# Hybrid two-layer decoder trunk on one core: where the cross-attention of layer 0 is done, and through which weight slots the out tiles go

## The reference

```python
h   = rmsnorm(x, norm1[i])
# one projection h @ w_in[i]; 768 columns wide for the mixer, 256 for the cross-attention queries
mix = mlstm(...)     # layer 0: 4 heads of 192, after a causal convolution of 4 taps and SiLU on q and k
mix = diff_attn(...) # layer 1: 6 heads, rotary, two softmaxes each
# memory cross-attention, 4 heads of 64:
q = rmsnorm(xq heads, q_norm);  k, v = rmsnorm(mem, mem_norm) @ w_mem_kv, k with rmsnorm
s = q k^T / 8;  pr = softmax(s);  xo = pr v
x = x + concat([mix, xo]) @ w_out[i]
x = x + SwiGLU(rmsnorm(x, norm2[i]))     # 2816 hidden
```

## Time and profile before

| | us |
|---|---|
| median of 3 runs | 1277.99 (1277.84 to 1279.39) |
| the profiled execution | 1277.5 |
| its span, first to last instruction | 1275.7 |
| TensorE busy | 1251.7 (98%) |
| VectorE, ScalarE, POOL busy | 530.2, 335.9, 857.3 |
| granted TensorE clock, mean | 0.996 |

### The profile page before, as it was taken

How to read it: one execution, slowest core, us unless ns; L and a number is a source line. 1 busy time by engine, 2 the same in 40 slices (tenths; PEclk the granted TensorE clock), 3 DMA queues, 4 the chain that set the end, 5 groups by cost and what they waited for, 6 DMA issues and landing times.

```text
span 1275.7 us, 15861 instructions
## 1 busy us (share of the span) xinstructions
PE 1251.7 (98%) x5762; PEld 1004.6 (79%) x5762; DVE 530.2 (42%) x788; ACT 335.9 (26%) x669; POOL 857.3 (67%) x1032
## 2 busy tenths in 40 slices
PE   7999999899999999999999999999999999999999
PEld 6888777678888888888877777777788888888887
DVE  6954434555332222213364777773723213321221
ACT  6422435633220011101131555553322001100110
POOL 7898432268777777777786344455678777777775
PEclk9999999899999999999999999999999999999999
DMA  7233111113222222223233222221222333222222
GB/s 257 97 129 116 50 50 50 33 57 100 99 99 99 99 99 91 92 97 99 74 124 100 83 67 65 60 62 63 83 85 96 99 99 99 94 99 90 96 78 103
DMA packets 34481, 115.90 MB, mean 91 GB/s; under 512 B 4349, under 2 KB 4862, under 8 KB 34302
## 3 DMA queue, kind: packets, MB, share of 16 engines
q1 hardware_dynamic: 32688, 111.16, 26.4%
q10 hardware_dynamic: 1742, 4.10, 1.2%
HBM read 110.00 MB, written 2.10 MB: 88 GB/s over the span
## 4 chain that ended last, share of the span: by engine, by line
PE 93%; DVE 2%; ACT 2%; POOL 1%; issue 1%; ACTq 0%; DMA 0%; SPq 0%; DVEq 0%; POOLq 0%
PE PS L1483 91%; POOL w_lo L528 1%; PE PS L1847 1%; DVE nmB L1390 0%; ACTq L840 0%; ACT V L771 0%; DMA w_raw<-in_wt_dram 0%; PE PS L1873 0%; POOL w_hi L523 0%; DVE nmA L1244 0%; PE PS L1677 0%; ACT PB L875 0%; DVE PS L1388 0%; PE PS L1544 0%; PE PS L1802 0%
## 5 line engine op out<-in xcount | busy, mean ns | idle before, releaser
L528 POOL TENSOR_TENSOR w_lo<-w_raw,w_hi 128x256 fp32r<-128x256 f32 x804 | 631.8, 816 | 17.1
L523 POOL TENSOR_SCALAR w_hi<-w_raw 128x1024 fp32r<-128x1024 f32 (+2 forms) x205 | 213.3, 1041 | 387.4 <-PE PS L1483 386.9
L1483 PE MATMUL PS<-Hh,w_hi 128*128 128x512 f32 x1072 | 430.9, 402 | 9.4 <-POOL w_lo L506 6.9
L1483 PE MATMUL PS<-Hh,w_lo 128*128 128x512 f32 x1072 | 418.6, 390 | 0.0
L1483 PE MATMUL PS<-Hl,w_hi 128*128 128x512 f32 x1072 | 418.4, 390 | 0.0
L1483 PEld LDWEIGHTS PS<-Hh,w_hi 128*128 128x128 f32 x1072 | 201.8, 188 | 64.1 <-issue 22.7
L1483 PEld LDWEIGHTS PS<-Hh,w_lo 128*128 128x128 f32 x1072 | 201.6, 188 | 42.8
L1483 PEld LDWEIGHTS PS<-Hl,w_hi 128*128 128x128 f32 x1072 | 202.0, 188 | 38.5 <-issue 1.0
L1483 PE MATMUL PS<-Ah,w_hi 128*128 128x512 f32 (+1 forms) x544 | 209.3, 385 | 3.6 <-POOL w_lo L528 2.9
L1483 PE MATMUL PS<-Ah,w_lo 128*128 128x512 f32 (+1 forms) x544 | 205.6, 378 | 0.0
L1483 PE MATMUL PS<-Al,w_hi 128*128 128x512 f32 (+1 forms) x544 | 205.5, 378 | 0.0
(11 more groups left out here) (257 smaller groups left out, 988.4 us busy)
## 6 DMA issues: line engine op xcount, KB each, us to landing
w_raw<-in_wt_dram SPq DMA_DIRECT2D x181, 512.0 KB, 3.3
w_raw<-in_wt_dram SPq DMA_DIRECT2D x16, 384.0 KB, 3.0
w_raw<-in_wt_dram SPq DMA_DIRECT2D x8, 448.0 KB, 3.2
QKR<-QKP ACTq DMA_DIRECT2D x24, 128.0 KB, 4.4
xT<-in_x_t_dram SPq DMA_DIRECT2D x8, 256.0 KB, 5.9
out_dram<-xT SPq DMA_DIRECT2D x8, 256.0 KB, 2.0
mT<-in_mem_t_dram SPq DMA_DIRECT2D x1, 1024.0 KB, 9.5
cn<-in_constants_dram ACTq DMA_DIRECT2D x1, 580.5 KB, 5.9
```

The source lines that it names most:

```text
L523: nc.gpsimd.tensor_scalar(w_hi[:, sl, 0:nk], w_raw[:, raw, 0:nk], 0.0, 1.0, ALU.add, ALU.mult).then_inc(w_round, 1)
L528: lo = nc.gpsimd.tensor_tensor(w_lo[:, sl, w], w_raw[:, raw, w], w_hi[:, sl, w].bitcast(F32), ALU.subtract)
L1483: return nc.tensor.matmul(out_, a, b, start=start, stop=stop)
```

## The change

1. The list of projections puts q9, q10, q11, x0, x1 at the end; v4 and v5 become tiles 26 and 27, the dense tiles of head 0. The transposes of v4 come in head 0's second tile, those of v5 in head 1's first. The sums of squares of the cross queries come in head 0 instead of head 3.
2. Each of the four cross-attention heads is done by itself (`m_` functions in the place of the `cross_` ones): scores of head x after block k=3 of the second dense tile of mLSTM head x; transposes after k=2 and value products after k=5 of the first dense tile of the next mLSTM head. The last one has its transposes and value products in the first and the second out tile. The normalising is on DVE alone.
3. The out tiles 34, 35 and 36 are opened with rows 0 to 3 and 6, then closed with rows 4, 5 and 7; the others follow whole. These tiles rotate through three slots. In layer 1, tile 130 goes to slot 2, 131 to 137 alternate between 0 and 1, and the extra tile is split behind tile 134.

```diff
 def slot_of(n):
-    return n % SPLIT if n < T_XA else n % 2
+    if n < T_HEAD:
+        return n % SPLIT
+    if T_OUT[0] <= n < T_OUT[0] + KD:
+        return (T_OUT[0] % 2, 1 - T_OUT[0] % 2, 2)[(n - T_OUT[0]) % 3]
+    if n < T_OUT[1]:
+        return n % 2
+    return 2 if n == T_OUT[1] else (n + 1) % 2

 def used_for(n):
-    return n - 2 if n < T_XA else n - 1
+    if n == T_OUT[0] + 2:
+        return T_HEAD
+    return n - 2 if n < T_HEAD or T_OUT[0] + 3 <= n < T_OUT[0] + KD else n - 1
...
# POOL
-                if T_OUT[1] + 2 <= n < T_OUT[1] + 2 + OPEN:
+                if T_OUT[1] <= n < T_OUT[1] + 3:
+                    pool.wait_ge(dense_done, T_HEAD if n == T_OUT[1] else n - 2)
+                elif T_OUT[1] + 3 <= n < T_OUT[1] + KD:
                     pool.wait_ge(out_open, n - T_OUT[1] - 1)
...
-                if n == T_OUT[1]:
+                if n == T_OUT[1] + OPEN - 1:
                     pool.wait_ge(z_in, 16)
+                    pool.wait_ge(out_open, 1)
...
# ACT
+            cross_sq(0, 0)
+            cross_sq(0, 1)
             for h in range(MH):
                 head_weights(h)
-                if h == 0:
+                if h == 1:
                     v_out(5)
                 if h == MH - 1:
                     out_gate(0, DONE_MC)
+                if h >= 1:
+                    m_pt(h - 1)
+                    m_hi(h - 1)
+                if h == MH - 1:
                     mixer_hi(0, DONE_MC)
                 head_num(h)
-                if h == MH - 2:
-                    cross_sq(0, 0)
-                    cross_sq(0, 1)
-                if h == MH - 1:
+                if h == 0:
+                    v_out(4)
                     cross_std(0)
                 head_std(h)
                 head_high(h)
+                m_exp(h)
             out_gate(DONE_MC, MC)
+            m_pt(MH - 1)
             mixer_hi(DONE_MC, MC)
-            cross_hi(1)
+            m_hi(MH - 1)
...
# DVE
             for h in range(MH):
                 head_diag(h)
                 head_p(h)
+                if h >= 1:
+                    m_p(h - 1)
                 if h == MH - 1:
                     mixer_out(0, DONE_MC)
-                scaled_out(*fill[2 * h])
+                if h >= 1:
+                    m_lo(h - 1)
+                fill_out(2 * h)
                 if h == MH - 1:
                     mixer_lo(0, DONE_MC)
                 head_cols(h)
+                if h == 0:
+                    cross_rq(0)
+                m_max(h)
                 if h == MH - 1:
-                    scaled_out(*fill[2 * h + 1])
-                    cross_rq(0)
+                    fill_out(2 * h + 1)
                 head_out(h)
                 if h < MH - 1:
-                    scaled_out(*fill[2 * h + 1])
+                    fill_out(2 * h + 1)
+            m_p(MH - 1)
             mixer_out(DONE_MC, MC)
             mixer_lo(DONE_MC, MC)
-            cross_lo(1)
+            m_lo(MH - 1)
...
+            def m_p(x):
+                r = rsA[:, 4 * x:4 * x + 4]
+                dve.wait_ge(ms_exp, 4 * x + 4)
+                nc.vector.reciprocal(r, r).then_inc(ms_rec, 1)
+                dve.wait_ge(ms_rec, x + 1)
+                for t in range(NT):
+                    nc.vector.tensor_scalar(M_P[t], M_P[t], r[:, t:t + 1], None, ALU.mult).then_inc(mp_ready, 1)
...
# PE
+            def m_s(x):
+                r = 64 * (x % 2)
+                if x == 0:
+                    pe.wait_ge(xq_std, 1)
+                    pe.wait_ge(v_ready, V_DONE[4])
+                else:
+                    pe.wait_ge(mt_ready, 2 * x)
+                    pe.wait_ge(mo_ready, x)
+                for t in range(NT):
+                    last = mm(PS[:, M_BANK[t // 2], (t % 2) * MEM:(t % 2 + 1) * MEM], xqA[r:r + 64, x // 2, t * P:(t + 1) * P],
+                              xk[r:r + 64, 0, x // 2])
+                    if t % 2:
+                        last.then_inc(ms_done, 1)
+            def m_t(x):
+                if x < MH - 1:
+                    pe.wait_ge(p_ready, NT * (x + 1) + 2)
+                pe.wait_ge(mp_ready, 4 * x + 4)
+                for mt in range(MT_TILES):
+                    for t in range(NT):
+                        last = nc.tensor.transpose(PS[:, M_BANK[mt], t * P:(t + 1) * P], M_P[t][:, mt * P:(mt + 1) * P], ident)
+                    last.then_inc(mt_done, 1)
...
             for h in range(MH):
                 def in_first(k):
-                    if h == 0 and k == 2:
-                        v_tr(MC - 1)
-                    if h == MH - 1 and 3 <= k < 3 + NT:
+                    if h == 0 and 3 <= k < 3 + NT:
                         cross_ss(0, 0, k - 3)
                         cross_ss(0, 1, k - 3)
+                    if h == 1 and k == 1:
+                        v_tr(5)
+                    if h >= 1 and k == 2:
+                        m_t(h - 1)
+                    if h >= 1 and k == 5:
+                        m_pv(h - 1)
                 def in_second(k):
+                    if h == 0 and k == 1:
+                        v_tr(4)
+                    if k == 3:
+                        m_s(h)
...
-            a_tile(T_OUT[0], ready=lambda k: [(mix_lo, k + 1)] if k < MC else [(xo_ready, k - MC + 1)])
-            a_tile(T_OUT[0] + 1)
-            with pe.Fori(1, KD // 2) as i:
-                a_tile(T_OUT[0], i)
-                a_tile(T_OUT[0] + 1, i)
+            out_blocks(0, (0, 1, 2, 3, 6), after=lambda i: m_t(MH - 1) if i == 2 else None)
+            out_blocks(1, (0, 1, 2, 3, 6), after=lambda i: m_pv(MH - 1) if i == 2 else None)
+            out_blocks(2, (0, 1, 2, 3, 6))
+            for j in range(3):
+                out_blocks(j, (4, 5, 7))
+            for j in range(3, KD):
+                out_blocks(j, range(KD))
```

More of the change, by code:

```diff
@@ L332, in hybrid_trunk @@
         xq_std = sem("xq_std")
[L333 to L343, removed]
+        ms_done = sem("ms_done")
+        ms_max = sem("ms_max")
+        ms_exp = sem("ms_exp")
+        ms_rec = sem("ms_rec")
+        mp_ready = sem("mp_ready")
+        mt_done = sem("mt_done")
+        mt_ready = sem("mt_ready")
+        mo_done = sem("mo_done")
+        mo_hi = sem("mo_hi")
+        mo_ready = sem("mo_ready")
         cs_done = sem("cs_done")
@@ L1140, in _ @@
             mem_out(7)
-            v_raw(4)
             k_norm(1)
@@ L1202, in head_out @@
                                         ALU.mult).then_inc(hout, 1)
-            dve.wait_ge(vtr_out, 2)
-            fill = [(T_XA, xqA[:, 0]), (T_XA + 1, xqA[:, 1])] + [(T_O + c, SO[:, c]) for c in range(MC)]
             def cross_rq(l):
@@ L1707, in _ @@
                 head_scores(h)
-                h_tile(fill[2 * h], after=in_first)
+                h_tile(T_HEAD + 2 * h, after=in_first)
                 head_pv(h)
-                h_tile(fill[2 * h + 1], after=in_second)
-            def cross_s(c):
-                for b in range(4):
-                    r = 64 * (b // 2)
-                    for a in range(2):
-                        t = 2 * (b % 2) + a
-                        last = mm(PS[:, X_BANK[c] + b, a * MEM:(a + 1) * MEM], xqA[r:r + 64, c, t * P:(t + 1) * P],
-                                  xk[r:r + 64, 0, c])
-                    last.then_inc(xs_done, 1)
@@ L1755, in _, with out_blocks @@
-            a_tile(T_OUT[0] + 1)
-            with pe.Fori(1, KD // 2) as i:
-                a_tile(T_OUT[0], i)
-                a_tile(T_OUT[0] + 1, i)
+                h_tile(T_HEAD + 2 * h + 1, after=in_second)
+            def out_blocks(j, rows, after=None):
+                n = T_OUT[0] + j
+                sl, bank = slot_of(n), out_bank(0, j)
+                if rows[0] == 0:
+                    pe.wait_ge(w_split, n + 1)
+                    if j == 2:
+                        pe.wait_ge(hn_low, 2 * MH)
+                        pe.wait_ge(hn_high, 2 * MH)
+                    else:
+                        pe.wait_ge(dense_free, freed_for(n))
+                for i, k in enumerate(rows):
+                    pe.wait_ge(*((mix_lo, k + 1) if k < MC else (mo_ready, 2 * (k - MC) + 2)))
+                    mm(PS[:, bank], w_hi[:, sl, k], Ah[:, k], start=k == 0, stop=False)
+                    mm(PS[:, bank], w_hi[:, sl, k], Al[:, k], start=False, stop=False)
+                    last = mm(PS[:, bank], w_lo[:, sl, k], Ah[:, k], start=False, stop=k == KD - 1)
+                    if k == KD - 1:
+                        last.then_inc(dense_done, 1)
+                    if after:
+                        after(i)
@@ L2014, in weight_tiles @@
         else:
-            put(n, aw, 0, i * P if kind == "q" else 2 * MIX + i * P)
-    for j in range(2):
-        put(T_XA + j, aw, 0, XQ_COL_A + j * P)
+            put(n, aw, 0, {"q": 0, "v": 2 * MIX, "x": XQ_COL_A}[kind] + i * P)
+    for c in range(4, MC):
+        put(v_number(c), aw, 0, 2 * MIX + c * P)
     for j in range(MC):
```

199 lines of the change are left out of this document (82 added, 117 removed).

## The result

The changed kernel takes 1280.93 us (median of 20 runs, the lowest 1278.97) where the kernel before takes 1277.91 beside it (20 runs): ratio 1.0023, 95% interval 1.0017 to 1.0030. It is slower by 3.0 us. One of the 20 runs was disturbed (1371.76 us at a mean clock of 0.871); it is left out of all that follows, and the median of the other 19 is 1280.61. The forecast was no change (1277.7), the range ended at 1280.8.

The account below looks back on a forecast made before the run. TensorE, busy 98% of the span, was taken as the bound. Layer 0's +3.1 us and layer 1's -3.4 gave -0.3 on the profiled 1277.5, which lies 0.5 under the median: 1277.7 us, range 1273.4 to 1280.8.

Parts of the forecast that it names:

- The clock at the new waits: Layer 0's new TensorE waits were priced without clock falls; falls had followed waits of 1.92 and 2.93 us, not 1.01.
- rival C: Clock falls at the new waits, 1.5 us each: 1279.2 with one in layer 0, up to 1282.2; chance 0.18.
- The stage goes, the heads cost 20.3: Layer 0: removing the lone cross-attention saves 20.9 us plus a 0.86 wait; four heads inside dense tiles cost 20.3.
- Rival A: Layer 0's inserted cross products keep the separate stage's rates, 12.5 us instead of 20.3: total 1269.9; chance 0.08.
- Weighing the pair against the lone head: Layer 0's cross products: a head standing alone loses the overlap of array halves; keeping it would save 7.8 us.
- The start, -0.13: Ahead of layer 0's heads: the last x tile's eviction replaces the SiLU wait, scores start at 144.53, saving 0.13 us.
- Head 0's wait, +1.0: Layer 0, cross-attention scores of head 0: TensorE waits for ScalarE's chain to the square root, +1.0 us (0 to 1.3).
- The last head's wait, +2.5: Layer 0, first out tile: last head's transposes wait for VectorE's four scalings beside POOL, +2.5 us (0.9 to 3.5).
- The fourth out tile, +1.15: Layer 0: the fourth out tile waits for POOL to split its weights into the first tile's slot, +1.15 us (0.2 to 1.6).
- Layer 0, +3.1: Sum of all layer 0 savings, head costs and new waits: +3.1 us; bounds of the waits alone give +0.1 to +4.9.
- Layer 1, -3.4: Third out tile's 2.93 us POOL wait goes, a 1.2 ScalarE wait comes, clock kept: -3.4 us (-1.9 if it falls).
- Rival B: Layer 0's new waits do not come, 4.65 us less there: total 1273.0; chance 0.14.

Follow-up runs that it names:

- the kernel without the three waits: Changed kernel with last head's products one out tile later, head 0's scores later, and no wait for x1's conversion, heads still alone: 1274.23 us, ratio 0.9966.
- The pairing: Changed kernel with each insertion taking both heads of a chunk for half of the tokens, computation complete: 1274.8 us, ratio 0.9976; with the three waits also removed, 1267.44 us.
- alternating halves: Changed kernel with each head's products put in turn into both row or column halves of the array, computation not kept: 1274.27 us, ratio 0.9967.

## Why the prediction was wrong

The time came 3.2 us over the forecast. 1.3 of it stands in the run without a fall (1278.97 against 1277.7), 2.0 are falls (the median over that run). The parts:

- **The clock at the new waits: the step that failed.** The sum of layer 0 gave its three new waits no fall, and rival C, one fall, got 0.18 and the price 1279.2. Of 19 runs 18 have one or two, by their mean clocks. My ground was that 1.01 us had left the clock at 1.00 and that only 1.92 and more had not; I drew a line at 2 us between them. The runs show no such line. In the changed kernel's trace a wait of 0.94 has a fall 1.2 us behind its end; 2.84 and 2.90 have none in the traces of two other kernels; the identical kernel has 0, 1 or 2. The mechanism of C stands in this: with the three waits there are falls in 18 of 19 runs, without them in none of 15. Its point of decision doesn't. Its price of 1.5 for each was about right (1.6 and 1.7).
- **The stage goes, the heads cost 20.3.** The bunches came as taken: 1.92 from start to start for scores, 1.86 for values. Rival A is out. The sum was nearly right: about 20.6. From head 0's first product to the fourth out tile the changed kernel needs 136.84 us; less its waits (1.03, 3.06 and 0.89, taken from start to start with the restart) and its two falls (3.3) that is 128.56. The kernel before has 129.30 there, less 21.76 for the stage and the wait behind it, plus 0.44 for the moved transposes, so 107.98 without heads. The difference is 20.6, 0.3 over the step. In the kernel without the three waits the same reckoning gives 21.05, of which 0.37 is a wait for POOL at its second out tile, which TensorE there reaches sooner.
- **Weighing the pair against the lone head.** The step took the loss of the overlap at 7.8. The pairing measured 6.8 without falls, and 6.7 and 7.1 between groups of equal clock (6.1 between the medians). The Trainium skill (TensorE: Matmul & The Clock Gate, Part 3, The mechanism) says that products in different halves can run at once; the trace agrees, 1.13 against 1.99 for eight passes, and does so with the halves alternating inside one dense tile, which the step had not thought of: it took the choice between 12.5 and 20.3 as the change's only two, when a third arrangement gets most of it back.
- **The start, -0.13.** The wait of 1.01 for ScalarE's SiLU did become one of 0.94 for the x1 tile's conversion. Head 0 started at 144.84, 0.3 later than taken; with the same wait it was 145.16 and 145.66 in two other traces. This may be scatter from the start of the program, where TensorE's waits for POOL differ from trace to trace (at 19 us 0.47 and 1.68 in those two, none in this one); it wasn't followed further.
- **Head 0's wait, +1.0:** 0.95. The chain on ScalarE is as written down: copies at 164.57, table load, square root at 166.55.
- **Heads 1 to 3, 0:** no wait in any trace.
- **The last head's wait, +2.5:** 2.84, and 3.0 from start to start. The four scalings took 3.23, not 2.7, and started 0.1 late against the turned head. The Trainium skill (SBUF — State Buffer, SBUF: two separate sides) has VectorE's two-port operations and GpSimd keep each other out for whole instructions, by which the wait would be nearer to 3.5. The rows agree with it more than with my 0.64 a piece: 0.81 each, beside pieces of POOL of 0.71 each. ScalarE, in the same place, needed 1.71.
- **The fourth out tile, +1.15:** 0.72, and 0.89 from start to start, because POOL's remainders took 3.45 beside VectorE and not 3.71.
- **Layer 0, +3.1:** +7.3 in the profiled execution, of which two falls are 3.3 (6.28 - 4.58 for the 16 passes, which took 4.58 in the trace without the x1 wait, and 1.6 at 262.04, against the same products in the trace with head 0's scores late). Without them +4.0. The lines above give 3.1 + 0.3 (start) + 0.3 (heads) + 0.6 (last head's wait with its restart) - 0.3 (fourth tile) = 4.0.
- **Layer 1, -3.4:** -2.9 at this place in the profiled execution, -2.6 with the two waits in the FFN. The wait was 1.63 and not 1.2, since the exponentials ahead of ScalarE's copy, which wait for VectorE, came 0.4 late against the third out tile. POOL splits weights beside them in both traces (from 866.60 before, from 874.33 here), so what made the 0.4 isn't shown. The two FFN waits (0.3 to 0.4 more) had no term. And 1.5 of the gain was a fall of the clock that does not come in every order of the kernel, nor in every run: with layer 0 changed, the old layer 1 costs only 0.7 to 0.8 more. What I took for a property of this place was one of the execution as a whole.
- **Rival B** (the waits don't come) is out: all three came, 4.5 us with POOL's against 4.65.

So the sum for a run without falls, corrected, is 1277.7 + 0.9 for layer 0 + 0.5 to 0.8 for layer 1 = 1279.1 to 1279.4 (measured 1278.97, one run), and the median adds one fall or two.

**Open.** Which wait is followed by a fall, in which execution, isn't settled: with none of the three waits it was 0 runs of 15, with one of 0.95 it was 1 of 10, with 0.94 and 0.95 5 of 11, with 0.94 and 2.84 5 of 11, with 0.95 and 2.84 9 of 11, with 0.94, 0.95 and 1.31 5 of 11, with all three 18 of 19 (and 10 of 10 in the paired kernel, 6 of 6 with alternating halves). So the share grows with the waits, but not in the order of their summed length, and waits of 1.36 and 1.63 in layer 1 had none behind them. No run here moved a wait of fixed length in time alone, and none changed what TensorE does just before a wait; either could be what decides.

## What to carry to other kernels

When a stage that stood alone is spread into others, price its products in the company they will have: pieces that shared the array's halves lose that overlap when one head is taken at a time, and can have it back if each insertion takes half of the tokens of two heads. Put an inserted piece one tile or some blocks later than its inputs' expected time; here three such edits of order took 4.7 us of waits and up to two clock falls of some 1.6 away, and the pairing 6.8 more. And give a chance, not a threshold, to a fall of the clock behind a wait: look at the run list's clocks beside the one trace.

## What the runs showed of the hardware

- The same program has 0, 1 or 2 stretches of 3.41 us at half clock, and its time steps by 1.4 to 2.0 us with each; the three kernels with no TensorE wait above 0.73 us in layer 0 behind the first weights spread over 0.6 to 0.7 us (1267.14 to 1267.7, for one), the change over 4.1.
- Waits of 2.84 and 2.90 us left the clock at 1.00 in some traces, one of 0.94 and one of 0.95 did not in others; waits of 1.36 and 1.63 in layer 1 have no fall behind them in any trace of the kernels that have them.
- Eight f32 passes of 64x256: 1.99 us in one row half, 1.13 alternating between both. Value passes of 128x512 with 64 columns: a pair in different column halves starts 0.01 apart and takes 0.64.
- Four scalings of 128x256 f32: 1.14 us on VectorE with POOL idle, 3.23 beside POOL, in one and the same trace; 1.71 on ScalarE beside POOL.
